# Two output projections and their layer norms, taken over the tokens in two halves instead of at once

## The chip, the core and the metric

The kernel runs on one core of one Trainium2 chip (trn2). The metric is the device time of one execution in microseconds (us). Work is spread over TensorE (PE), VectorE (DVE), ScalarE (ACT), GpSimd (POOL) and the DMA queues, which SyncE (SP) issues here. The engines run on their own instruction lists and meet at semaphores.

## What is computed

Two transformer blocks over 1024 tokens of width 1024, in float32. The part that matters is the end of each of the two layers of the second block:

```python
def mixer_sublayer(x, mem, w_in, w_mem_kv, w_out, main_fn):
    ...
    y = jnp.concatenate([y_main * jax.nn.silu(g_main), y_mem * jax.nn.silu(g_mem)], axis=-1)
    return y @ w_out                      # (1024 x 1536) @ (1536 x 1024)

def second_block(...):
    for layer in range(2):
        if layer == 1:
            k_sh, v_sh, cum_sh = shared_kv(x, w_kv_shared, b_forget)   # x @ w_kv_shared first
        y = mixer_sublayer(x, mem, w_in[layer], w_mem_kv[layer], w_out[layer], main_fn)
        x = layer_norm(ALPHA * x + y, ln_g[layer], ln_b[layer])        # over the 1024 features
```

## The kernel before

Activations lie feature-major in SBUF: 128 features by 1024 tokens is one tile, so a layer norm over the features needs sums over partitions, which PE makes. Every float32 operand is kept as two parts, `hi` and `lo` (names `whi`/`wlo` for weights, `Yb` for the input of the output projection, `Hb` for x), and each product is three matmuls (`mm3`, L327 to L329). A matmul moves 512 tokens, so a weight block of 128x128 is used for two groups of three matmuls.

Weights come as one stream of panels of 128x1024 (eight 128x128 blocks). SP loads panel q into `raw[q % 2]` once panel q-2 is split (`load_panel`, L371). POOL splits it into `whi[q % 2]` and `wlo[q % 2]` (`split`, L672 and L674) once PE is done with panel q-2 (`panel_done`). PE waits for `split`. So the buffers are two deep at each of the three steps, and POOL is at most one panel ahead of the one that PE uses.

`out_proj(l)` appears once in each engine's program. PE (from L1118) makes eight output tiles of 128 features by 1024 tokens from 12 panels; a tile takes 12 blocks, so tiles end in the middle or at the end of a panel (semaphores `out_mid` and `panel_done`). Tile t goes to PSUM pair `G[t % 2]`, and PE may start tile t only when tile t-2 has been taken out (`g_free`). Ahead of it DVE makes the twelve tiles of `Yb_lo` (L1794), and tile 0 waits for them one by one (`yb_lo`).

DVE (from L2191) takes each tile out of PSUM into `Z` and adds ALPHA * x. From tile 3 on, x less a shift row is prepared one tile ahead (`ahead`, L2210 and L2212), so that the take-out is one addition. Then come a running sum (`add_sum`) and a running sum of squares (`add_square`), ACT making the squares. For one tile n of 3 to 6, DVE's list is in this order:

```python
tt(Z[:, n, :], g, Z[:, n, :], ALU.add, free)     # take-out, reads PSUM and SBUF
add_sum(n)                                       # two SBUF inputs
ahead(n + 1)                                     # two instructions, two SBUF inputs each
add_square(n)                                    # two SBUF inputs
```

After tile 7 the norm follows: PE sums over the partitions (L1145), DVE makes mean and variance, ACT the root, PE spreads them to rows (L1151), ACT copies the rows to SBUF (`acc`, `rs`), and DVE and ACT go over the eight tiles: `centred`, `scaled`, ACT's gain and bias, and in layer 0 the split into `Hb_hi` (ACT) and `Hb_lo` (`low`, DVE). In layer 1 ACT's result is stored (`out<-Z`). After layer 0 PE goes on with `token_values(0)`, the shared values: for each of four panels, eight token tiles of 128 tokens (`VORDER`), each to its own PSUM bank, each needing `Hb` of two feature tiles; it waits for `ap_lo`.

The order of instructions on each engine is that of the program text; nothing reorders it.

Of the kernel before, what the change touches and what calls it, by code (L numbers as in the profile page):

```python
# [40 lines left out]
for _name, _w in (("c", 8), ("cc", 8), ("ada_b", 48), ("n1", 8), ("n2", 8), ("b_gate", 16), ("qng", 2),  # L41
# [7 lines left out]
          ("mem", 16), ("mlp", 64), ("pool", 20), ("mem1", 8), ("out1", 12), ("foxv", 4), ("forget", 1), ("foxw", 4), ("fox", 24), ("mem2", 8), ("out2", 12))  # L49
P0 = {}  # L50
_n = 0
for _name, _w in PANELS:
# [3 lines left out]
NP = _n + STREAM_GAP  # L56
# [4 lines left out]
         ("mem1", 16), ("out1", 8), ("mem2", 16), ("out2", 8))  # L61
# [63 lines left out]
VORDER = (tuple(range(8)), (2, 3, 4, 5, 6, 7, 0, 1))  # L125
# [5 lines left out]
def build(nc, d, out, upto=99, dbg=None):  # L131
    ctx = ExitStack()
    with ctx:
# [227 lines left out]
        def sp_program(sp):  # L361
            def load_panel(stage, per, i, j):

                if isinstance(i, int):
                    j, i = j + per * i, 0
                n = P0[stage] + LEAD + j
                q = n + per * i

                sp.wait_ge(S("split"), q - 1)
                for to, of in placed(raw[n % 2], q) if isinstance(i, int) else [(raw[n % 2][:, :], d["w"][q + STREAM_GAP])]:  # L370
                    sp.dma_start(to, of).then_inc(S(f"loaded{n % 2}"), 16)  # L371

            def stream(q):

                if q < P0["gates"]:
                    return 16 + q
                if q < P0["mem"]:
                    return 16 + STREAM_GAP + q
                return STREAM_GAP + q if q >= P0["mlp"] else q - P0["mem"]

            def placed(buf, q):
# [17 lines left out]
                if q < P0["foxv"] or q >= P0["mem2"]:  # L399
                    return [(buf[:, :], d["w"][stream(q)])]  # L400
                w0 = P0["foxv"] + STREAM_GAP
                q += STREAM_GAP
                if q == P0["forget"] + STREAM_GAP:
                    return [(buf[:, :], d["w"][w0])]
                if q < P0["fox"] + STREAM_GAP:
                    n, a = (q - w0, w0 + 3) if q < w0 + 4 else (q - w0 - 5, w0 + 19)
                    return [(buf[:, :].rearrange("p (t c) -> p t c", t=4), d["w"][a:a + 13:4].rearrange("t p c -> p t c")[:, :, 256 * n:256 * n + 256])]
                m = q - STREAM_GAP - P0["fox"]
# [183 lines left out]
            def out_proj(l):  # L592
                st = f"out{l + 1}"
                for j in range(12):
                    load_panel(st, 12, 0, j)
# [53 lines left out]
            if on("out2"):  # L649
                out_proj(1)  # L650
                for k in range(KT):
                    sp.wait_ge(S("ln2_out"), k + 1)
                    sp.dma_start(out[k], Z[:, k, :]).then_inc(S("out_stored"), 16)
                sp.wait_ge(S("out_stored"), 16 * KT)
# [4 lines left out]
        def pool_program(gp):  # L659
# [55 lines left out]
            for stage, per, n in (("mem1", 4, 2), ("out1", 6, 2), ("foxv", 4, 1), ("forget", 1, 1), ("foxw", 4, 1), ("fox", 24, 1), ("mem2", 4, 2),  # L715
                                  ("out2", 6, 2)):
# [8 lines left out]
        def pe_program(pe):  # L725
# [392 lines left out]
            def out_proj(l):  # L1118
                st = f"out{l + 1}"
                have = -1  # L1120
                for t in range(KT):
                    if t == 3:
                        pe.wait_ge(S("ln_sh"), 5 * l + 1)
                        for h in range(2):
                            last = nc.tensor.matmul(ps[:, (4 + h) * HALF:(5 + h) * HALF], onesr[:, :], accr[:, h * HALF:(h + 1) * HALF], start=True, stop=True)
                        last.then_inc(S("ln_sh"), 1)
                    o = pair(pe, st, 8, 0, t)
                    b = 12 * t
                    while b < 12 * t + 12:
                        j = b // 8  # L1130
                        if j != have:
                            wh, wl = panel(st, 12, 0, j)
                            have = j
                        e = min(8 * j + 8, 12 * t + 12)
                        last = blocks(o, wh, wl, Yb[0], Yb[1], range(b - 8 * j, e - 8 * j), b == 12 * t, e == 12 * t + 12, k0=b - 12 * t,
                                      ready=(lambda k: pe.wait_ge(S("yb_lo"), MT * l + k + 1)) if t == 0 else None)
                        if e == 8 * j + 8:
                            done(last)
                        else:
                            last.then_inc(S("out_mid"), 1)  # L1140
                        b = e
                for n, src in enumerate((acc, dsq)):
                    pe.wait_ge(S("ln_acc"), 14 * l + 13 + n)
                    for t in range(KT):
                        last = nc.tensor.matmul(ps[:, (4 + n) * HALF + t:(4 + n) * HALF + t + 1], src[:, P * t:P * t + P], onesf[:, 0:1], start=True, stop=True)  # L1145
                    last.then_inc(S("ln_pe"), 1)
                for n, (b, col_) in enumerate(((6, mean), (4, var))):
                    pe.wait_ge(S("ln_col"), 4 * l + (1, 4)[n])
                    for t in range(KT):
                        c = b * HALF + P * t  # L1150
                        last = nc.tensor.matmul(ps[:, c:c + P], col_[:, t:t + 1].to_broadcast([P, P]), ident[:, :], start=True, stop=True)  # L1151
                    last.then_inc(S("ln_pe"), 1)
# [3 lines left out]
            if on("out1"):  # L1156
                out_proj(0)
            if on("forget"):
# [4 lines left out]
                def token_values(hf):  # L1163
                    st = ("foxv", "foxw")[hf]
                    for n in range(4):
                        wh, wl = panel(st, 4, 0, n)
                        for x, tt in enumerate(VORDER[hf]):
                            if n == 0 and hf == 0 and tt == 4:
                                pe.wait_ge(S("ln_sh"), 5)
                            if n == 0 and hf == 1:  # L1170
                                if tt >= 2:
                                    pe.wait_ge(S("fx_vlo"), 2 * tt + 2)
                                else:
                                    pe.wait_ge(S("logits_read"), 1)
                            for k in range(2):
                                kt = 2 * n + k
                                if hf == 0 and x == 0:
                                    pe.wait_ge(S("ap_lo"), 24 + kt + 1)
# [8 lines left out]
                pe.wait_ge(S("fx_vlo"), 4)  # L1187
# [123 lines left out]
            if on("out2"):  # L1311
                out_proj(1)
# [6 lines left out]
        NORM = {"n1": 0, "latkv": 1, "n2": 2, "ln0": 3, "ln1": 4}  # L1319
        APPLY = {"n1": 0, "n1c": 8, "n2": 16, "ln0": 24, "ln1": 32}  # L1320
# [44 lines left out]
        def act_program(act):  # L1365
# [290 lines left out]
            def out_proj(l):  # L1656
# [7 lines left out]
                act.wait_ge(S("ln_v"), 24 * l + 1)  # L1664
                copy(accr[:, :], Z[:, 0, :], S("ln_sh"))
                act.wait_ge(S("ln_sh"), 5 * l + 2)
                copy(rs[:, 0:T], ps[:, 4 * HALF:6 * HALF], S("ln_sh"), scale=1.0 / P)
                for k in range(KT):
                    if k < 3:
                        act.wait_ge(S("ln_v"), 24 * l + 4 + k)  # L1670
                    else:
                        evicted(act, st, 8, 0, k)
                    if k >= 2:
                        act.wait_ge(S("ln_acc"), 14 * l + 2 * max(k - 2, 1))
                    copy(tmp[k % 2][:, 0:T], Z[:, k, :], S("ln_sq"), ACT.Square)
# [871 lines left out]
```

## Time and profile before

| | |
|---|---|
| Time, median of 3 runs | 3466.75 us (3466.52 to 3469.32) |
| Profiled execution: its time, its span | 3461.23 us, 3459.4 us |
| PE matmul busy | 3136.3 us, 91% of the span |
| DVE busy | 1531.2 us, 44% |
| ACT busy | 911.9 us, 26% |
| POOL busy | 1082.7 us, 31% |
| Mean granted TensorE clock | 0.964 |
| Output projection of layer 0: first to last matmul | from 2287.58 us to 2420.49 us of the span |
| Output projection of layer 1, the norm and the stores | from 3288 us to the end |

Busy shares are averages over stages with different limits. The lines named with an instruction are those of the kernel text. The span runs from the first to the last instruction; the execution's own time is 1.83 us more than the span.

### The profile page before, as it was taken

How to read it: one execution, taken by the hardware profiler on the slowest of the kernel's cores; microseconds unless marked ns; L12 is line 12 of the kernel's file. 1: busy time of each engine (PE TensorE's matmuls, PEld its weight loads, DVE VectorE, ACT ScalarE, POOL GpSimd, SP SyncE). 2: the span in 40 equal slices, each digit the busy share in tenths (PEclk: the TensorE clock that was granted, in tenths of full speed). 3: DMA queues.
4: the chain of work that ended last, by engine and by line, in shares of the span. 5: the costliest groups of instructions: out<-in, count | busy, mean ns of one | idle time of the engine just before them, and what ended most of it. 6: DMA issues, size and time to landing. Idle time of an engine off the chain costs nothing.

```text
span 3459.4 us, 38319 instructions
## 1 busy us (share of the span) xinstructions
PE 3136.3 (91%) x15303; PEld 2619.8 (76%) x15303; DVE 1531.2 (44%) x2168; ACT 911.9 (26%) x1470; POOL 1082.7 (31%) x482
## 2 busy tenths in 40 slices
PE   6979998999889899999999899979899999989797
PEld 6768776888767688888887677658788787867585
DVE  1952212888544331313132343445535656562455
ACT  1322211666212210101011101220334555451212
POOL 0332255000135744434443333214331122211132
PEclk9979998999999999999999999989899999999898
DMA  5343444222142311111111111101241121111012
GB/s 209 129 136 108 170 141 151 65 71 59 67 152 73 122 49 50 49 50 49 50 49 43 49 43 55 43 19 49 64 133 56 50 62 49 56 42 45 24 38 85
DMA packets 114165, 259.37 MB, mean 75 GB/s; under 512 B 46768, under 2 KB 64768, under 8 KB 110032
## 3 DMA queue, kind: packets, MB, share of 16 engines
q1 hardware_dynamic: 113744, 256.95, 22.8%
q8 instruction: 122, 2.00, 0.2%
q14 instruction: 43, 0.35, 0.0%
q10 hardware_dynamic: 256, 0.07, 0.0%
HBM read 214.54 MB, written 42.38 MB: 74 GB/s over the span
## 4 chain that ended last, share of the span: by engine, by line
PE 68%; issue 16%; DVE 8%; POOL 4%; ACT 3%; DMA 1%; POOLq 0%; SPq 0%; DVEq 0%; ACTq 0%
PE ps L327 20%; PE ps L328 20%; PE ps L329 20%; POOL whi L672 2%; PE ps L1272 2%; ACT tmp L1367 2%; DVE tmp L2350 2%; POOL wlo L674 2%; PE ps L769 2%; PE ps L1258 1%; DVE Z L1797 1%; DVE ETb_lo L1794 1%; DMA adaE<-in_ada 1%; PE ps L1115 1%; DMA raw<-in_w 0%
## 5 line engine op out<-in xcount | busy, mean ns | idle before, releaser
L672 POOL TENSOR_TENSOR whi<-raw,onesf 128x1024 fp32r<-128x1024 f32 x235 | 455.6, 1939 | 2308.2 <-PE ps L329 2229.4
L674 POOL TENSOR_TENSOR wlo<-raw,whi 128x1024 fp32r<-128x1024 f32 x235 | 615.2, 2618 | 18.4
L327 PE MATMUL ps<-Hb_hi,whi 128*128 128x512 f32 x1424 | 569.0, 400 | 18.2 <-DVE Y L2135 5.8
L329 PE MATMUL ps<-Hb_hi,wlo 128*128 128x512 f32 x1424 | 555.8, 390 | 0.0
L328 PE MATMUL ps<-Hb_lo,whi 128*128 128x512 f32 x1424 | 555.3, 390 | 0.0
L327 PEld LDWEIGHTS ps<-Hb_hi,whi 128*128 128x128 f32 x1424 | 268.1, 188 | 75.0 <-issue 18.0
L329 PEld LDWEIGHTS ps<-Hb_hi,wlo 128*128 128x128 f32 x1424 | 267.5, 188 | 57.1
L328 PEld LDWEIGHTS ps<-Hb_lo,whi 128*128 128x128 f32 x1424 | 268.3, 188 | 50.0
L1367 ACT ACTIVATE tmp<-ps 64x256 f32<-64x256 f32 (+1 forms) x120 | 81.6, 680 | 654.4 <-PE ps L329 584.8
L1367 ACT ACTIVATE tmp<-tmp,mx 128x1280 f32<-128x1280 f32 (+2 forms) x192 | 187.1, 974 | 107.0 <-DVE mx L2350 89.2
L327 PE MATMUL ps<-Uhi,whi 128*128 128x512 f32 x512 | 199.2, 389 | 0.0
L328 PE MATMUL ps<-Ulo,whi 128*128 128x512 f32 x512 | 199.2, 389 | 0.0
L329 PE MATMUL ps<-Uhi,wlo 128*128 128x512 f32 x512 | 199.2, 389 | 0.0
L327 PE MATMUL ps<-Yb_hi,whi 128*128 128x512 f32 x384 | 151.3, 394 | 36.0 <-DVE Yb_lo L1794 36.0
L2095 DVE SCALAR_TENSOR_TENSOR X<-ps,modx,X 128x1024 f32<-128x1024 f32 x32 | 41.1, 1284 | 286.5 <-PE ps L329 286.5
L1797 DVE TENSOR_TENSOR tmp<-tmp 128x1024 f32<-128x1024 f32 x32 | 64.3, 2008 | 202.0 <-ACT tmp L1367 202.0
L328 PE MATMUL ps<-Yb_lo,whi 128*128 128x512 f32 x384 | 150.7, 392 | 0.0
L329 PE MATMUL ps<-Yb_hi,wlo 128*128 128x512 f32 x384 | 150.6, 392 | 0.0
L327 PE MATMUL ps<-Hhi,whi 128*128 128x512 f32 x320 | 127.6, 399 | 9.9 <-DVE Hlo L1331 9.9
L328 PE MATMUL ps<-Hlo,whi 128*128 128x512 f32 x320 | 126.1, 394 | 0.0
L329 PE MATMUL ps<-Hhi,wlo 128*128 128x512 f32 x320 | 126.0, 394 | 0.0
L1258 PE MATMUL ps<-ident,tmp 128*128 128x128 f32 x576 | 88.9, 282 | 28.9 <-ACT tmp L1367 28.8
(403 smaller groups left out, 6088.7 us busy)
## 6 DMA issues: line engine op xcount, KB each, us to landing
raw<-in_w SPq DMA_DIRECT2D x221, 512.0 KB, 3.3
adas<-in_ada SPq DMA_DIRECT2D x16, 1024.0 KB, 4.9
raw<-in_w SPq DMA_DIRECT2D x36, 256.0 KB, 4.0
adaE<-in_ada SPq DMA_DIRECT2D x4, 2048.0 KB, 25.3
gate_d<-gst SPq DMA_DIRECT2D x16, 512.0 KB, 2.9
v_d<-VS SPq DMA_DIRECT2D x2, 4096.0 KB, 14.3
ncB<-cum_d SPq DMA_DIRECT2D x16, 512.0 KB, 3.7
Vx<-v_d SPq DMA_DIRECT2D x16, 512.0 KB, 4.5
```

The lines of the kernel that those rows point to most:

```text
L327: nc.tensor.matmul(o, wh, xh, start=start, stop=False)
L328: nc.tensor.matmul(o, wh, xl, start=False, stop=False)
L329: return nc.tensor.matmul(o, wl, xh, start=False, stop=stop)
L672: nc.gpsimd.tensor_tensor(whi[b][:, 0:w], raw[b][:, 0:w], onesf[:, 0:1].to_broadcast([P, w]), ALU.mult).then_inc(S("split_hi"), 1)
L674: nc.gpsimd.tensor_tensor(wlo[b][:, 0:w], raw[b][:, 0:w], f32(whi[b][:, 0:w]), ALU.subtract).then_inc(S("split"), 1)
L769: last = nc.tensor.matmul(ps[:, c:c + 2], adaE[g][:, n // 2, k, P * (n % 2):P * (n % 2) + P], silc[:, :].rearrange("p (x k) -> p k x", k=K ...
L1258: last = nc.tensor.transpose(ps[:, b + P * (kt - 4 * x):b + P * (kt - 4 * x) + P], tmp[qt % 2][:, P * kt:P * kt + P], ident[:, :])
L1272: last = nc.tensor.matmul(ps[:, 5 * HALF + c0:5 * HALF + CTX], Vx[h % 2][:, kt, :], E[x][:, kt, c0:CTX], start=kt == 0 and x == 0, stop=kt ...
L1367: nc.scalar.activation(dst, src, func, **kw).then_inc(sem, 1)
L1797: nc.vector.tensor_tensor(o, a, b, op).then_inc(sem, 1)
L2095: nc.vector.scalar_tensor_tensor(X1[:, k, :], g, modx[:, 40 + k:41 + k], X1[:, k, :], ALU.mult, ALU.add).then_inc(free, 1)
L2350: nc.vector.tensor_tensor_reduce(tmp[qt % 2][:, c0:c1], ps[:, b:b + c1 - c0], ncB[:, c0:c1], -1.0, col_ if x else 3e38, ALU.add, ALU.min, ...
```

## The change

Both output projections run over the tokens by halves of 512 (`x` = 0, 1). The numbers of panels and tiles double, and the second half's panels are the same weights loaded and split again:

```diff
-... ("out1", 12), ... ("out2", 12))        # PANELS
+... ("out1", 24), ... ("out2", 24))
-... ("out1", 8), ... ("out2", 8))          # TILES
+... ("out1", 16), ... ("out2", 16))
-VORDER = (tuple(range(8)), (2, 3, 4, 5, 6, 7, 0, 1))
+VORDER = ((1, 3, 0, 2, 4, 5, 6, 7), (2, 3, 4, 5, 6, 7, 0, 1))
+BESIDE = {3: (0, 1), 4: (2, 3), 5: (4, 5), 6: (6,), 7: (7,)}
```

A panel now serves 24 matmuls instead of 48. PE's program:

```diff
+                def token_sums(x):          # over the partitions, for 4 token tiles
+                    for n, src in enumerate((acc, dsq)):
+                        pe.wait_ge(S("ln_acc"), 14 * (2 * l + x) + 13 + n)
+                        ... 4 matmuls of 128x1
+                def rows(x, n):             # n = 0 mean, n = 1 inverse deviation
+                    pe.wait_ge(S("ln_col"), 4 * (2 * l + x) + (1, 4)[n])
+                        ... 4 matmuls of 128x128
+                for x in range(2):
+                    X = [y[:, :, HALF * x:HALF * x + HALF] for y in Yb]
                     for t in range(KT):
+                        if t == 3:
+                            shift_row(x)
+                        if x and t == 1:
+                            token_sums(0)
+                        if x and t == 2:
+                            rows(0, 0)
+                            rows(0, 1)
+                        o = pair(pe, st, 16, 0, 8 * x + t)
...
+                yield
+                token_sums(1)
+                yield
+                rows(1, 0)
+                yield
+                rows(1, 1)
+                yield
```

In layer 0 the last three steps stand between the first four token tiles of `token_values(0)`, which belong to half 0 (order 1, 3, 0, 2); the other four wait for half 1 (`ap_lo` 24 + 2 * x + kt + 1 for x = 0 and 4). In layer 1 they follow each other. DVE's program (`first` is the take-out of tiles 0 to 2, all operations are 512 wide):

```diff
+                for x in range(2):
+                    first(x, 0)
+                    if x:
+                        moments(0)
+                    first(x, 1)
+                    if x:
+                        inverse(0)
+                    first(x, 2)
+                    if x:
+                        for k in range(3):
+                            centred(0, k)
...
+                    for n in range(3, KT):
+                        g, free = arrive(x, n)
+                        tt(Z[:, n, c], g, Z[:, n, c], ALU.add, free)
+                        add_sum(x, n)
+                        if n + 1 < KT:
+                            ahead(x, n + 1)
+                        add_square(x, n)
+                        if x:
+                            for k in BESIDE.get(n, ()):
+                                scaled(0, k)
+                                if k + 3 < KT:
+                                    centred(0, k + 3)
+                                if k:
+                                    low(0, k - 1)     # layer 0 only
+                low(0, KT - 1)
+                moments(1)
+                inverse(1)
...
```

ACT's program has the same order: squares of half 0, `factors(0)` (root and the two row copies), squares of half 1 with gain and bias (and `Hb_hi`) of half 0 beside them by `BESIDE`, `factors(1)`, the rest of half 1. SP loads 24 panels instead of 12 in each projection and stores the result in 16 pieces of 256 KB instead of 8 of 512 KB, the first eight as soon as half 0 is ready. POOL splits the 24 panels with the same two instructions each. The twelve `Yb_lo` instructions at the start stay 1024 wide.

## Rows read from the trace of the kernel before

**Rows 1.** The page's chain of work that ended last, by engine.

```profile
PE 68%; issue 16%; DVE 8%; POOL 4%; ACT 3%; DMA 1%; POOLq 0%; SPq 0%; DVEq 0%; ACTq 0%
```

**Rows 2.** Busy time by stretch: us and (instructions) of each engine, clock, DMA.

```profile
2287.00:2298.00 11.00, 10.42 (x37) 8.49 (x38) 11.00 (x11) 3.23 (x4) 0.00 (x0) 0.78 0.00 0
2298.00:2421.00 123.00, 122.88 (x543) 101.40 (x541) 53.54 (x39) 9.53 (x9) 51.35 (x22) 1.00 0.17 48
2421.00:2450.00 29.00, 14.90 (x70) 13.35 (x71) 20.64 (x20) 11.62 (x12) 5.10 (x2) 0.69 0.09 20
3421.00:3460.00 39.00, 12.93 (x67) 11.93 (x65) 25.16 (x23) 14.49 (x14) 5.10 (x2) 0.64 0.31 122
```

**Rows 3.** PE in order of time, projection of layer 0 and what follows: start, us.

```profile
2287.58 0.77 PE L327 MATMUL ps<-Yb_hi,whi 128*128 128x512 f32 x1 [17.98 <-DVE Yb_lo L1794]
...
2420.49 0.39 PE L329 MATMUL ps<-Yb_hi,wlo 128*128 128x512 f32 x1
2424.05 2.75 PE L1145 MATMUL ps<-onesf,acc 128*128 128x1 f32 x16 [3.18 <-DVE acc L1797]
2427.34 3.57 PE L1145 MATMUL ps<-onesf,dsq 128*128 128x1 f32 x16 [0.54 <-DVE dsq L1797]
2430.77 3.76 PE L1151 MATMUL ps<-ident,stat 128*128 128x128 f32 x16
2436.07 2.05 PE L1151 MATMUL ps<-ident,stat_pool 128*128 128x128 f32 x16 [1.54 <-DVE stat_pool L2265]
2445.20 0.77 PE L327 MATMUL ps<-whi,Hb_hi 128*128 128x512 f32 x1 [7.08 <-DVE Hb_lo L1794]
...
2450.16 0.63 PE L327 MATMUL ps<-whi,Hb_hi 128*128 128x512 f32 x1
```

**Rows 4.** Groups of instructions from 2287 to 2421 us, shapes apart: busy, mean ns.

```profile
L674 POOL TENSOR_TENSOR wlo<-raw,whi 128x1024 fp32r<-128x1024 f32 x11 | 29.8, 2708 | 0.9
L672 POOL TENSOR_TENSOR whi<-raw,onesf 128x1024 fp32r<-128x1024 f32 x11 | 21.6, 1961 | 116.8 <-PE ps L329 116.8
L1794 DVE TENSOR_TENSOR Yb_lo<-Y,Yb_hi 128x1024 fp32r<-128x1024 f32 x12 | 13.7, 1220 | 0.0
```

**Rows 5.** POOL in order of time, in the projection of layer 1.

```profile
3334.14 1.90 POOL L672 TENSOR_TENSOR whi<-raw,onesf 128x1024 fp32r<-128x1024 f32 x1 [5.65 <-PE ps L329]
3336.11 2.39 POOL L674 TENSOR_TENSOR wlo<-raw,whi 128x1024 fp32r<-128x1024 f32 x1
3345.47 1.90 POOL L672 TENSOR_TENSOR whi<-raw,onesf 128x1024 fp32r<-128x1024 f32 x1 [6.97 <-PE ps L329]
3347.45 3.25 POOL L674 TENSOR_TENSOR wlo<-raw,whi 128x1024 fp32r<-128x1024 f32 x1
3356.36 1.90 POOL L672 TENSOR_TENSOR whi<-raw,onesf 128x1024 fp32r<-128x1024 f32 x1 [5.65 <-PE ps L329]
```

**Rows 6.** DVE in order of time, beside the last three rows of POOL.

```profile
3345.52 2.93 DVE L1797 TENSOR_TENSOR Z<-Z,rs 128x1024 f32<-128x1024 f32 x1
3348.37 3.41 DVE L1797 TENSOR_TENSOR dsq<-tmp 128x1024 f32<-128x1024 f32 x1
3351.70 1.21 DVE L1797 TENSOR_TENSOR acc<-acc,Z 128x1024 f32<-128x1024 f32 x1
3352.84 1.21 DVE L2210 SCALAR_TENSOR_TENSOR Z<-Hb_hi,rs 128x1024 f32<-128x1024 f32 x1
...
3356.36 1.22 DVE L1797 TENSOR_TENSOR Z<-ps,Z 128x1024 f32<-128x1024 f32 x1
```

**Rows 7.** Narrower operations of DVE and ACT over the whole span: busy, mean ns.

```profile
L1794 DVE TENSOR_TENSOR ETb_lo<-ps,ETb_hi 128x512 fp32r<-128x512 f32 x64 | 42.7, 688 | 15.9 <-ACT ETb_hi L1367 15.9
L1367 ACT ACTIVATE rs<-ps 128x512 f32<-128x512 f32 x8 | 4.7, 590 | 7.3 <-PE ps L329 7.2
```

**Rows 8.** ACT and DMA at the end of layer 1; weight loads of the page.

```profile
3452.51 3.51 ACT L1367 ACTIVATE Z<-Z,cols 128x1024 f32<-128x1024 f32 x3 [1.03 <-DVE Z L1797]
raw<-in_w SPq DMA_DIRECT2D x221, 512.0 KB, 3.3
```

More of the change, by code:

```diff
@@ L1119, in out_proj @@
                 st = f"out{l + 1}"
-                have = -1
[L1121 to L1141, printed above, removed]
@@ L1142, in out_proj, with shift_row @@
-                for n, src in enumerate((acc, dsq)):
-                    pe.wait_ge(S("ln_acc"), 14 * l + 13 + n)
-                    for t in range(KT):
[L1145 to L1152, printed above, removed]
+                def shift_row(x):
+                    pe.wait_ge(S("ln_sh"), 8 * l + 2 * x + 1)
+                    nc.tensor.matmul(ps[:, 4 * HALF:5 * HALF], onesr[:, :], accr[:, HALF * x:HALF * x + HALF], start=True, stop=True).then_inc(S("ln_pe"), 1)
@@ L1156, in pe_program @@
             if on("out1"):
-                out_proj(0)
+                norm = out_proj(0)
+                next(norm)
             if on("forget"):
@@ new lines, in low @@
+                def low(x, k):
+                    if l:
+                        return
+                    c, _ = half(x)
+                    dve.wait_ge(S("ap_hi"), APPLY[f"ln0{x}"] + k + 1)
+                    sub(Hb[1][:, k, c], tmp[k % 2][:, c], Hb[0][:, k, c], S("ap_lo"))
+                for x in range(2):
+                    first(x, 0)
[8 more added lines that the diff above has]
+                            centred(0, k)
+                    dve.wait_ge(S("ln_v"), 16 * (2 * l + x) + 3)
+                    dve.wait_ge(S("ln_sh"), 8 * l + (2, 6)[x])
+                    shifted(x, 0)
+                    shifted(x, 1)
+                    add_sum(x, 1)
+                    shifted(x, 2)
+                    add_square(x, 1)
+                    add_sum(x, 2)
+                    ahead(x, 3)
+                    add_square(x, 2)
+                    for n in range(3, KT):
+                        g, free = arrive(x, n)
+                        c, m = half(x)
+                        dve.wait_ge(S("ln_v"), 16 * m + 2 * n + 2)
+                        tt(Z[:, n, c], g, Z[:, n, c], ALU.add, free)
[10 more added lines that the diff above has]
+                                    low(0, k - 1)
@@ L2293, in dve_program @@
+                low(1, KT - 1)
             if on("mem1"):
```

298 lines of the change are left out of this document (174 added, 124 removed).

## Prediction, made before the changed kernel ran

> **What bounds the kernel now.** I read the page's chain first: PE holds 68% of it [rows 1], so TensorE sets most of the time. Then the windows around the edit. In the 123 us of the projection PE has work without a gap, at the full clock, while POOL works 51.4 us and DVE 53.5 us [rows 2]. In the 29 us behind it and in the last 39 us PE is half idle, and the clock falls to 0.69 and 0.64 [rows 2]: these are the two norm tails, the only thing near the edit that a change can win.
>
> The time line of PE gives their size [rows 3]. From the first matmul (2287.58) to the end of the last issue (2420.49 + 0.23) are 133.1 us. 12 panels of 48 matmuls are 576; at 5.45 us for 24 (0.227 us each, the rate that is left when some 2 us of cold start and shift row are taken off) they make 131 us. PE then works steadily again only at 2450.16, with six matmuls (1.4 us) done before: 28 us lost. In layer 1 from 3421.3 to 3459.4: 38.1 us to the end.
>
> The view that decides is DVE beside POOL, in order of time. POOL's `wlo` takes 2.39 us alone and 3.25 with DVE at work [rows 5]. DVE's additions of two SBUF inputs take 1.14 us from start to start, but 2.93 and 3.41 us when POOL works [rows 6]. The ends fit to the tenth: `whi` runs to 3347.37, DVE's addition that started at 3345.52 ends at 3348.45, 1.08 us later; `wlo` ends at 3350.70, DVE's next at 3351.78, again 1.08 later [rows 5, 6]. So the two don't run at once: they take turns, one instruction each. An addition that reads PSUM beside `whi` took its plain 1.22 us at 3356.36 [rows 5, 6]. Before, this cost nothing, since POOL needs 4.4 us of each 10.9 us panel.
>
> **The prices.** POOL: 24 panels by 1.90 + 2.39 = 4.3 us are 103 us per projection, for 12 panels before 52. PE uses up a panel in 5.45 us, so POOL alone keeps pace, with 1.1 us to spare. Loading a panel takes 3.3 us [rows 8] and has one split's time (4.4 us or more) before it is needed, so the 12 added loads of 512 KB lie hidden; uncovered they would cost 3.3 us for the first only.
>
> DVE: a 512-wide operation isn't in the trace with two SBUF inputs. The upper bound is 0.69 us, the one with a PSUM input [rows 7]; the lower is half of 1.14, 0.57. I take 0.60 alone, 0.55 in a turn between two POOL instructions, 0.65 for a take-out from PSUM. ACT: 0.59 [rows 7] for half of 1024, where 0.5 would be half: small, and ACT has room.
>
> Port turns per projection: 103 (POOL), 12 Yb_lo by 1.08 = 13, and DVE's two-input instructions: per half 3 (second step of the take-out), 3 shifted, 7 sums, 7 sums of squares, 10 ahead = 30, and 16 of the norm (24 in layer 0 with `low`): 92 and 108 by 0.55 = 51 and 59. In all 167 and 175 us. Before the same sum was 52 + 13 + 46 or 54 by 1.08 = 115 and 123, in a window (first matmul to last DVE step) of 167 and 181 us. So the port that DVE and POOL take turns at goes from two thirds full to all of it. The change can't win much even if it packed perfectly.
>
> **How it runs.** I went through the four lists by hand, with PE 5.45 us a panel, POOL 1.90 and 2.39, DVE as above; t counts from the first matmul of the projection.
>
> Start: tile 0 needs twelve Yb_lo. They come 1.14 us apart [rows 4], and a block now lasts 0.68 us instead of 1.36, so PE waits for DVE. Panel 0 is done at 8.8; POOL then splits panel 2 and takes two turns between the last four Yb_lo. Tile 0 ends at 17.5, where 12 blocks and the cold start would be 9.7: +7.8.
>
> Half 0: POOL is busy nearly throughout, so DVE gets two turns in a panel, three in a tile (1.5 panels, 8.2 us), and it needs four: add_sum, two ahead, add_square. It falls behind. Tiles 0 to 2 leave ten turns behind the take-out of tile 2 (its second step, 3 shifted, 2 sums, 2 squares, 2 ahead), due before the take-out of tile 3, for which tile 5 waits: PE stands from 50.5 to 54.8: +4.3. While PE stands POOL has nothing to split, and DVE catches up; tiles 6 and 7 just fit. Half 0 ends at 79.3.
>
> Between the halves: token_sums(0) is due after tile 8, at 88.2. DVE then still has the end of half 0 before it (take-out of tile 7 at 91.5, the last sum at 92.1). PE's sums were 2.75 and 3.57 us for eight token tiles [rows 3], half of that now, and are over at 95.8: +7.6. The rows: half of 3.76 and 2.05 us plus a wait for the inverse, which is queued behind the take-out of tile 9: +3.9.
>
> Half 1: to the four turns of a tile come scaled, centred and low, twice in tiles 3 to 5: 9, 10 and 9 turns where POOL leaves three. PE stands before tiles 13 and 14 of 16 for psum pairs, 6.5 us each: +13. Tile 15 meets a DVE that has caught up but is then 14 turns behind once more. The last matmul comes 36.6 us later than before, at t = 170 in layer 0, and some 2.4 us earlier than that in layer 1, which has no low.
>
> Tail of layer 0: behind the last matmul DVE still has those 14 turns with POOL's last split between them. The last sums are in at 184.9, PE's sums end at 187.5, rows at 190.8 and 193.2 (token tiles between), the first Hb_lo of half 1 at 196.4, the second at 198.3. PE has done 27 matmuls (6.2 us) there, so it lost 28 - 6 = 22 us, against 28 before: -6. Layer 0: 36.6 - 6.3 = +30. Tail of layer 1: sums at 183, rows at 186.5, the last scaled at 195.5, ACT 0.8, and as before 3.4 us from ACT's end (3456.0 [rows 8]) to the end of the span: 199.7 against 171.2 before: +28.5. Standing 3 us or more has also brought the 1.2 GHz clock back (0.63 us instead of 0.39 at 2450.16) [rows 3], about 1.5 us each time; since DVE and POOL gain what PE loses, I count +3 in all.
>
> Sum: 30 + 28.5 + 3 = +61 on the profiled execution's 3461.23 us. This execution lies 5.5 us below the median of the runs; a difference holds on either, so 3466.75 + 61 = 3528; I take 3526, since the waits in the walk were rounded up.
>
> The Trainium skill has a rule on this, and it speaks against the change: SBUF — State Buffer, section "Who interferes with whom", says that a DVE instruction with two SBUF inputs contends with a GpSimd instruction that reads SBUF, that the later one waits for the whole of the earlier one, and that one SBUF input does not contend. The rows on both sides agree. If the take-outs from PSUM contended too, 16 more turns of 0.55 us would be added per projection, some 18 us in both.
>
> **Rivals.**
> A, forecast: turns at the port, DVE behind, PE waits for PSUM pairs: +61, own range +35 to +90.
> B, the lists pack well: PE's waits are filled, and only the port's sum counts. Window 167 or 175 us plus about 6 us in which nobody can use it (panel 0 to 2, wait for PE at t = 15 to 20) and the 3.4 us of stores: +5 in layer 1 and 0 to +10 in layer 0; with the start's +7.8 half seen in each, +13 to +23 (3480 to 3490). For it: DVE does catch up whenever PE stands. Against: POOL has no work in just these waits, so port time is lost.
> C, other side, one mechanism: 512-wide steps slip into POOL's 1.1 us of slack per panel and DVE keeps up. It decides at DVE finishing a tile's work within 8.17 us. Then the costs are 3.6 (Yb_lo paces tile 0: 13.3 for 9.7), 5.2 of PE's inserted sums and rows, 1.5 of waiting: +10.3; the tails shrink to half a norm: -16 in layer 0, -13 in layer 1. Together -8: 3459. For it: the tails are really long. Against: 4.3 + 3 by 0.55 us a panel is more than 5.45.
> D, POOL becomes PE's bound: a turn of DVE costs POOL 0.87 us as the 1024-wide one did (3.25 less 2.39) whatever its width. A panel takes 4.3 + 1.7 = 6.0 us, 0.6 by 22 by 2 = 26 us more than A: +87, 3554. Against: the wait should shrink with the width.
>
> **How the numbers follow.** A 0.64, B 0.15, C 0.08, D 0.08, and 0.05 that gains and costs meet within 0.2% (7 us, about what a measurement tells from no change). Range: from the upper part of B (+19) to D (+87): 3486 to 3554. Outside lie C, no change, half of B's chance, and a little of A's and D's ends, 0.2 to 0.25 in all. Faster by over 0.2%: 0.05 (most of C), same 0.06, slower 0.89.
>
> **What would show it.** Two groups of 24 splits between the first and last Yb matmul instead of 12; POOL busy around 100 us of some 170. DVE's 512-wide two-input steps averaging well over 1 us in the projection. PE waiting for Yb_lo inside tile 0, for DVE's take-out (Z<-ps) several times by 4 to 7 us, and about 7 us before the sums of half 0. First to last matmul of the projections 160 to 180 us instead of 133. The tail of layer 0 about as long as before, that of layer 1 some 7 us shorter. The prediction is wrong if PE has no gaps before tiles 5, 13 and 14, or if 512-wide steps beside POOL take under 0.8 us.

## Result and profile after

| | before | after |
|---|---|---|
| Time, median (range), same chip | 3468.03 us (3466.52 to 3473.71) | 3508.01 us (3505.46 to 3509.36) |
| Ratio to before | | 1.0111 [1.0094, 1.0129] |
| Profiled execution: its time, its span | 3461.23, 3459.4 us | 3509.36, 3507.5 us |
| First to last Yb matmul, layer 0 / layer 1 | 133.1 / 132.7 us | 166.9 / 163.1 us |
| First Yb matmul of layer 0 to that of layer 1 | 1001.1 us | 1025.1 us |
| First Yb matmul of layer 1 to the end of the span | 170.8 us | 190.2 us |
| POOL busy, whole span | 1082.7 us | 1199.3 us |

The kernel became 40 us slower. In the profiled executions the spans differ by 48.1 us: 24.0 in layer 0, 19.4 in layer 1, and 4.7 ahead of the first Yb matmul of layer 0. Those 4.7 us are in stages that the change doesn't touch: over all kernels of this document that matmul starts anywhere from 2284.7 to 2294.1 us. So I compare by the two stages.

The page's chain of the changed kernel, by engine: beside [rows 1] PE has given 6 points away, 3 to issue and 2 to DVE.

```profile
PE 62%; issue 19%; DVE 10%; POOL 4%; ACT 3%; DMA 1%; POOLq 0%; SPq 0%; DVEq 0%; ACTq 0%
```

Windows of the changed kernel (columns as in [rows 2]): start, rest of the projection of layer 0, its tail, end of layer 1.

```profile
2292.00:2303.00 11.00, 10.06 (x30) 6.62 (x30) 11.00 (x11) 2.90 (x4) 1.85 (x1) 0.79 0.00 0
2303.00:2459.00 156.00, 139.07 (x582) 111.81 (x581) 116.17 (x97) 23.25 (x36) 109.22 (x46) 0.93 0.24 75
2459.00:2485.00 26.00, 16.69 (x68) 13.38 (x67) 20.08 (x30) 10.54 (x16) 4.99 (x2) 0.74 0.20 43
3468.00:3507.50 39.50, 17.18 (x68) 14.67 (x68) 31.16 (x39) 12.72 (x19) 10.91 (x5) 0.71 0.42 147
```

In the second line POOL is busy 109.2 us of 156 (51.4 of 123 before) and DVE 116.2 (53.5), though DVE's arithmetic grew only by the norm of one half. PE is no longer busy throughout: 139 of 156, at a granted clock of 0.93 instead of 1.00.

PE in order of time, layer 0 of the changed kernel: the places where it waited, and the four inserted steps.

```profile
2309.34 0.50 PE L331 MATMUL ps<-Yb_hi,whi 128*128 128x512 f32 x1 [1.01 <-POOL wlo L688]
2343.44 0.50 PE L331 MATMUL ps<-Yb_hi,whi 128*128 128x512 f32 x1 [3.39 <-DVE Z L1869]
2378.33 0.94 PE L1145 MATMUL ps<-onesf,acc 128*128 128x1 f32 x8
2379.13 1.03 PE L1145 MATMUL ps<-onesf,dsq 128*128 128x1 f32 x8
2388.33 1.05 PE L1152 MATMUL ps<-ident,stat 128*128 128x128 f32 x8
2391.22 1.20 PE L1152 MATMUL ps<-ident,stat_pool 128*128 128x128 f32 x8 [1.84 <-DVE stat_pool L2332]
2424.18 0.79 PE L331 MATMUL ps<-Yb_hi,whi 128*128 128x512 f32 x1 [5.34 <-DVE Z L1869]
2448.33 0.79 PE L331 MATMUL ps<-Yb_hi,whi 128*128 128x512 f32 x1 [4.97 <-DVE Z L1869]
2466.99 1.87 PE L1145 MATMUL ps<-onesf,acc 128*128 128x1 f32 x8 [6.38 <-DVE acc L1869]
2480.77 0.66 PE L331 MATMUL ps<-whi,Hb_hi 128*128 128x512 f32 x1 [2.43 <-DVE Hb_lo L1866]
```

A row starts where its wait ends. Three stops wait for DVE's take-out (`Z`): before tiles 5, 13 and 15 (180, 468 and 540 Yb matmuls lie ahead of them). Behind each the clock is at 1.2 GHz for a while (granted 0.59 from 2424 to 2431 us, 0.60 from 2448 to 2455); the matmuls behind the later two show 0.79 and 0.63 us instead of 0.39.

The groups of layer 0's projection, shapes apart (busy, mean ns), answer to [rows 4]:

```profile
L688 POOL TENSOR_TENSOR wlo<-raw,whi 128x1024 fp32r<-128x1024 f32 x23 | 60.9, 2647 | 1.8
L686 POOL TENSOR_TENSOR whi<-raw,onesf 128x1024 fp32r<-128x1024 f32 x23 | 50.2, 2183 | 95.4 <-PE ps L333 95.4
L1869 DVE TENSOR_TENSOR dsq<-dsq,tmp 128x512 f32<-128x512 f32 x10 | 18.4, 1845 | 0.0
L1869 DVE TENSOR_TENSOR acc<-acc,Z 128x512 f32<-128x512 f32 x11 | 17.6, 1596 | 0.3
L1869 DVE TENSOR_TENSOR Z<-ps,Z 128x512 f32<-128x512 f32 x9 | 6.1, 683 | 2.6 <-PE ps L333 2.6
```

Two SBUF inputs cost 1.6 to 1.85 us on average, one of them in PSUM 0.68, of the same width. The turns can be read one by one where DVE is behind, near tile 15, POOL first, then DVE:

```profile
2455.97 2.72 POOL L688 TENSOR_TENSOR wlo<-raw,whi 128x1024 fp32r<-128x1024 f32 x1
2459.39 2.32 POOL L686 TENSOR_TENSOR whi<-raw,onesf 128x1024 fp32r<-128x1024 f32 x1 [0.71 <-PE ps L333]
2461.79 2.67 POOL L688 TENSOR_TENSOR wlo<-raw,whi 128x1024 fp32r<-128x1024 f32 x1
2456.36 2.87 DVE L2294 SCALAR_TENSOR_TENSOR Z<-Hb_hi,rs 128x512 f32<-128x512 f32 x1
2459.88 2.38 DVE L1869 TENSOR_TENSOR dsq<-dsq,tmp 128x512 f32<-128x512 f32 x1
2462.18 2.82 DVE L1869 TENSOR_TENSOR tmp<-Z,rs 128x512 f32<-128x512 f32 x1
```

POOL's three end at 2458.69, 2461.71 and 2464.46, DVE's at 2459.23, 2462.26 and 2465.00: each time 0.54 or 0.55 us later, one 512-wide step. POOL pays 0.3 us for such a turn (2.72 and 2.67 against 2.39 [rows 5]).

### The profile page after: what moved, and what is told of

Same layout as the page of the kernel before. It is cut to its first block, busy times and chain, and to the rows that moved or that the text cites. A ratio compares the mean times of both kernels' runs of the same rounds, so it can differ in the third digit from the quotient of the medians.

```text
span 3507.5 us, 38701 instructions
## 1 busy us (share of the span) xinstructions
PE 3164.1 (90%) x15303; PEld 2630.7 (75%) x15303; DVE 1638.4 (47%) x2292; ACT 924.4 (26%) x1520; POOL 1199.3 (34%) x530
## 4 chain that ended last, share of the span: by engine, by line
PE 62%; issue 19%; DVE 10%; POOL 4%; ACT 3%; DMA 1%; POOLq 0%; SPq 0%; DVEq 0%; ACTq 0%
PE ps L331 19%; PE ps L332 18%; PE ps L333 18%; POOL whi L686 2%; PE ps L1313 2%; DVE Z L1869 2%; POOL wlo L688 2%; ACT tmp L1409 2%; DVE tmp L2463 2%; PE ps L783 1%; PE ps L1299 1%; DVE acc L1869 1%; DVE ETb_lo L1866 1%; DMA adaE<-in_ada 1%; PE ps L908 0%
## 5 line engine op out<-in xcount | busy, mean ns | idle before, releaser
L686 POOL TENSOR_TENSOR whi<-raw,onesf 128x1024 fp32r<-128x1024 f32 x259 | 511.8, 1976 | 2248.4 <-PE ps L333 2169.5
L688 POOL TENSOR_TENSOR wlo<-raw,whi 128x1024 fp32r<-128x1024 f32 x259 | 676.0, 2610 | 20.3
L331 PE MATMUL ps<-Yb_hi,whi 128*128 128x512 f32 x384 | 161.2, 420 | 65.9 <-DVE Yb_lo L1866 38.0
L1409 ACT ACTIVATE tmp<-tmp,mx 128x1280 f32<-128x1280 f32 (+2 forms) x192 | 187.1, 974 | 108.7 <-DVE mx L2463 90.7
L331 PEld LDWEIGHTS ps<-Yb_hi,whi 128*128 128x128 f32 x384 | 76.5, 199 | 95.1 <-issue 40.8
```

Of the source, the lines that this page charges most:

```text
L331: nc.tensor.matmul(o, wh, xh, start=start, stop=False)
L686: nc.gpsimd.tensor_tensor(whi[b][:, 0:w], raw[b][:, 0:w], onesf[:, 0:1].to_broadcast([P, w]), ALU.mult).then_inc(S("split_hi"), 1)
L688: nc.gpsimd.tensor_tensor(wlo[b][:, 0:w], raw[b][:, 0:w], f32(whi[b][:, 0:w]), ALU.subtract).then_inc(S("split"), 1)
L1409: nc.scalar.activation(dst, src, func, **kw).then_inc(sem, 1)
```

## Experiments

"Changed" below is the changed kernel, "before" the one before. Times are medians; each ratio is to before on the same chip. The two stages: P0 / P1 are first to last Yb matmul in layers 0 and 1; L0 and L1 the two stage times of the table above (changed: P 166.9 / 163.1, L 1025.1 / 190.2; before: P 133.1 / 132.7, L 1001.1 / 170.8). Before's own median beside these runs was 3464 to 3466 us for 1 to 5, 3471 for 6 to 9 and 3467 for 10 to 12, so a difference of two medians of different groups can be off by a few us; the stage times, from the profiled executions, are the closer comparison.

| kernel | us | ratio | P0 / P1 | L0 / L1 |
|---|---|---|---|---|
| 1 a_tiny | 3445.29 | 0.9947 [0.9930, 0.9964] | 140.7 / 140.7 | 990.9 / 161.4 |
| 2 b_split_twice | 3480.30 | 1.0050 [1.0034, 1.0067] | 139.8 / 139.3 | 1011.3 / 177.4 |
| 3 a_beside_end | 3506.11 | 1.0121 [1.0101, 1.0141] | 159.3 / 157.9 | 1025.0 / 187.5 |
| 4 a_yb_halves | 3508.98 | 1.0134 [1.0117, 1.0151] | 167.6 / 166.0 | 1025.0 / 191.4 |
| 5 b_norm_halves | 3465.36 | 0.9996 [0.9986, 1.0006] | 133.2 / 133.9 | 998.4 / 170.9 |
| 6 a_split_512 | 3497.93 | 1.0089 [1.0063, 1.0115] | 159.3 / 159.0 | 1020.6 / 184.5 |
| 7 a_narrow_squares | 3503.20 | 1.0100 [1.0075, 1.0125] | 163.3 / 158.1 | 1021.5 / 187.1 |
| 8 a_one_input_squares | 3498.30 | 1.0090 [1.0064, 1.0115] | 163.4 / 158.1 | 1021.6 / 187.1 |
| 9 a_act_hi | 3464.95 | 0.9990 [0.9978, 1.0002] | 150.0 / 147.5 | 1001.1 / 170.6 |
| 10 a_psum | 3474.44 | 1.0022 [1.0013, 1.0031] | 150.4 / 149.5 | 1010.4 / 171.4 |
| 11 a_psum_act_hi | 3463.35 | 0.9993 [0.9984, 1.0002] | 149.9 / 147.9 | 1001.1 / 168.8 |
| 12 b_act_hi | 3471.07 | 1.0013 [1.0004, 1.0022] | 133.1 / 132.7 | 1004.5 / 174.1 |

**1, changed without POOL's work.** The loads and waits stay, the split is 8 columns wide (the weights' other columns are left unsplit).

```diff
-split(P0[stage] + SPLIT_LEAD + j, i, per)
+split(P0[stage] + SPLIT_LEAD + j, i, per, 8 if stage in ("out1", "out2") else PW)
```

> The changed kernel, with POOL's two split instructions of the 48 panels of both output projections cut from 1024 to 8 columns (so most of the split weights of these panels are stale; panels, loads, semaphores and PE's matmuls are all there). Theory A, the port that POOL and DVE take turns at: the waits of PE for DVE's take-outs (3.4, 5.4 and 5.0 us in layer 0, 3.4, 5.4 and 3.2 in layer 1) vanish, and with them the cold clock behind them; the projection takes about 143 us instead of 167 and 163; the whole time falls by 45 to 55 us to 3455 to 3465, a little under the kernel before. Theory B, DVE's own work and the order of its list: the waits stay, and the time stays above 3495. Theory C, POOL alone too slow for PE's 5.45 us a panel: only the waits for wlo (1.0 us twice) vanish, 3505.

All of the loss is gone, and the kernel is 19 us faster than before; it came out 10 us under theory A's range. DVE's groups in layer 0's projection are at their plain duration:

```profile
L1869 DVE TENSOR_TENSOR acc<-acc,Z 128x512 f32<-128x512 f32 x11 | 7.6, 690 | 0.3
L1869 DVE TENSOR_TENSOR dsq<-dsq,tmp 128x512 f32<-128x512 f32 x11 | 7.5, 685 | 0.0
```

PE waited in no place over 0.7 us up to the end of the projection. What turns the halves into a loss is the split beside DVE. Without it they are about 10 us a layer ahead of before (990.9 for 1001.1, 161.4 for 170.8), with DVE's longer list and the doubled loads in it. That is an upper bound for what the halves are worth: before still makes its own 12 splits a projection, and it wasn't run without them.

**2, before with POOL's work doubled.** Each of the 24 splits of the projections is made twice.

```diff
+for _ in range(2): whi = raw * onesf; wlo = raw - whi      # only in stages out1, out2
```

> The kernel before, with each of the 24 splits of the two output projections made twice in a row on POOL: the doubled splitting alone, with no halves. POOL is then busy 8.7 of each 10.9 us. Theory A: in a tile of 16.3 us POOL takes 12.9 and DVE's four two-input steps 4.3 of the shared port, 17.2 together, so DVE falls behind by 1 us a tile and its steps average above 2 us; PE begins to wait late in the projection and the tails get longer: +10 to +25 us, 3478 to 3493. Theory B, the port doesn't matter: 0 to +3 us.

Theory A's range held (+16 us), but by another wait than in the changed kernel: here POOL is the one that PE waits for, four times a projection, and the tails hardly grew (3.5 us in layer 0, none in layer 1).

```profile
2358.69 0.47 PE L327 MATMUL ps<-Yb_hi,whi 128*128 128x512 f32 x1 [1.59 <-POOL wlo L680]
2370.93 0.50 PE L327 MATMUL ps<-Yb_hi,whi 128*128 128x512 f32 x1 [1.08 <-POOL wlo L680]
```

With 1024-wide steps beside them the splits average 2.9 (`wlo`) and 2.35 us (`whi`), 10.5 a panel of 10.9. The doubled splitting alone costs 6.7 and 6.6 us in the two projections, where the changed kernel lost 33.8 and 30.4. DVE has half as many steps here, each twice as wide, and so needs half the turns.

**3, the norm of half 0 not beside tiles 11 to 15 but behind tile 15.**

```diff
-BESIDE = {3: (0, 1), 4: (2, 3), 5: (4, 5), 6: (6,), 7: (7,)}
+BESIDE = {7: (0, 1, 2, 3, 4, 5, 6, 7)}
```

> The changed kernel with BESIDE = {7: all eight}: the norm's steps for half 0 stand behind tile 7 of half 1 instead of between its tiles. Theory A: the wait before tile 14 of 16 goes (5 us and 3 us, and 1.5 us of cold clock), the one before tile 13 stays, but 16 or 24 steps of 0.6 us now lie in the tail, ahead of the moments of half 1: 3505 to 3525. Rival, the interleaving is what costs: 3495 or less.

As theory A had it, nothing is gained: the projection ends 7.6 us sooner (the second late stop is gone), and PE then waits 8.65 us for the first token tiles. DVE's norm steps of half 0 were only put off; behind the last matmul they take their plain 0.68 us each.

```profile
2462.21 0.77 PE L331 MATMUL ps<-whi,Hb_hi 128*128 128x512 f32 x1 [8.65 <-DVE Hb_lo L1866]
```

**4, Yb_lo by halves**, the second twelve behind the take-outs of tiles 0 and 1.

```diff
-for f in range(MT): Yb_lo(f)                    # 1024 wide
+for f in range(MT): Yb_lo(0, f)                 # 512 wide
+first(0, 0); Yb_lo(1, 0..5); first(0, 1); Yb_lo(1, 6..11)
```

> The changed kernel with the twelve Yb_lo instructions made by halves too: 512 wide for half 0 ahead of tile 0, those of half 1 behind the take-outs of tiles 0 and 1, where DVE is idle. Theory: tile 0 is no longer paced by DVE (3.5 us a layer) and the first split of the projection doesn't wait for the row of Yb_lo (1 us): 7 to 9 us less, 3499 to 3501. Rival: the time is given back at the wait before tile 5, since the port is full: 0 to 2 us less.

The theory (7 to 9 us less) missed and the rival (0 to 2 us less) comes nearer: nothing was gained. The start became faster (the shift row came at t = 27.2 instead of 30.9 us, t counted from the first Yb matmul), and the next take-out later. The wait moved to tile 4:

```profile
2324.55 0.80 PE L331 MATMUL ps<-Yb_hi,whi 128*128 128x512 f32 x1 [3.54 <-DVE Z L2288]
```

**5, before with only its norm by halves**, projection untouched: sums of squares, rows and norm steps in pieces of 512.

```diff
+PIECES = [(x, 2 * n + k) for n in range(4) for x in range(2) for k in range(2)]
```

> The kernel before with its projection untouched (12 panels, split once), and only the norm behind it by token halves: sums of squares, mean and deviation rows and their copies for tokens 0 to 511 first, then centred, scaled, gain and bias and the split of x in pieces of 512 tokens, in the order half 0 of features 0 and 1, half 1 of features 0 and 1, half 0 of features 2 and 3, and so on; the token tiles wait for their own half. Theory: both tails get shorter since the row copies and the first pieces come earlier, with no work added for POOL: the first Hb_lo some 9 us earlier in layer 0, the end some 3 us earlier in layer 1: 8 to 15 us less, 3453 to 3460. Rival: the tail is paced by DVE's 24 and 16 steps, which are no shorter by halves: 0 to 4 us less.

Missed: 8 to 15 us less were expected, and the time is before's; it lies in the rival's range (0 to 4 us less), though not for the rival's reason alone (a tail paced by DVE's steps). The norm started sooner, as meant: PE's steady row begins at 2446.13, 19.6 us behind the last Yb matmul, where it was 29.7 before [rows 3]. Most of that was given back further on; 2.7 us of layer 0's stage are left. POOL, DVE and PE some 10 to 27 us later:

```profile
2456.77 13.93 POOL L675 TENSOR_TENSOR whi<-raw,onesf 128x1024 fp32r<-128x1024 f32 x1 [24.54 <-PE ps L329]
```
```profile
2468.27 0.68 DVE L1833 TENSOR_TENSOR tmp<-Z,rs 128x512 f32<-128x512 f32 x1
2469.29 4.71 DVE L1830 TENSOR_TENSOR Hb_lo<-tmp,Hb_hi 128x512 fp32r<-128x512 f32 x2 [0.34 <-ACT Hb_hi L1381]
```
```profile
2473.50 0.80 PE L327 MATMUL ps<-whi,Hb_hi 128*128 128x512 f32 x1 [6.00 <-POOL wlo L677]
```

`whi` (1.9 us of work) was given the port at 2470.70 - 1.90 = 2468.80 us, just when DVE's unbroken row of 512-wide steps ended (2468.95) because it had to wait for ACT. PE then stood 6 us for the panel. POOL had come at 2456.77; 20 steps of DVE, 0.60 us from start to start, began after that and went ahead of it.

**6, the same splits in four instructions of 512 columns.**

```diff
-tensor_tensor(whi[b][:, 0:w], ...); tensor_tensor(wlo[b][:, 0:w], ...)
+tensor_tensor(whi[b][:, s_], ...) for both halves s_ of w; the same for wlo
```

> The changed kernel, with each split of the two projections' stages made by four POOL instructions of 512 columns instead of two of 1024: the same weights, the same bytes, but DVE may take the port between any two of them. Turns by instruction (my theory): DVE gets up to four turns a panel, six a tile, and needs four in half 0, so the wait before tile 5 (3.4 us) goes and those before tiles 13 and 14 shrink to under 2 us; POOL pays for more turns and PE waits for wlo in small pieces. First to last Yb matmul 150 to 158 us instead of 167 and 163, total 3480 to 3498 us. Rival, the port is full and only the sum of port time counts, however it is cut: within 4 us of the changed kernel, 3504 to 3512 us.

At the upper end of the theory's range, 10 us better than changed (4.5 and 5.7 in the two stages); the projections, 159 us, missed the theory's 150 to 158. The wait before tile 5 is gone, six waits of 0.4 to 1.2 us for `wlo` came in half 0 of layer 0, and in half 1 three more of them came and two for the take-out stayed, of 1.0 and 4.8 us. The theory's "under 2 us" for the last missed; finer turns help DVE, but POOL pays for them (1.37 and 1.52 us for half a panel, 5.8 for a panel that PE uses up in 5.45).

```profile
L694 POOL TENSOR_TENSOR wlo<-raw,whi 128x512 fp32r<-128x512 f32 x46 | 69.1, 1521 | 1.8
L689 POOL TENSOR_TENSOR whi<-raw,onesf 128x512 fp32r<-128x512 f32 x46 | 62.1, 1369 | 69.2 <-PE ps L333 69.2
```

**7 and 8, changed with 12 of 14 additions of squares on 8 columns** (most of the sum of squares is left out): in 7 as additions of two SBUF inputs, in 8 as `tensor_scalar` of one.

```diff
-tt(dsq[:, c], dsq[:, c], tmp[n % 2][:, c], ALU.add, S("ln_acc"))
+tt(dsq[:, w], dsq[:, w], tmp[n % 2][:, w], ALU.add, S("ln_acc"))        # 7, w: 8 columns
+nc.vector.tensor_scalar(dsq[:, w], tmp[n % 2][:, w], 1.0, None, ALU.mult)   # 8
```

> The changed kernel with twelve of the fourteen additions to the running sum of squares in each projection done on 8 columns instead of 512 (that part of the sum of squares is left out; the instructions, their order and their two SBUF inputs stay). Turns by instruction: an addition of 8 columns still has to wait for POOL's instruction to end, so DVE is as far behind as before; it only gives back its own 0.5 us each, some 2 to 3 of which lie ahead of each of PE's waits. Waits before tiles 5, 13 and 14 each 0 to 1.5 us shorter, total 3498 to 3506 us. Rival, only port time counts: 12 by 0.55 us less in each projection, all seen in the time: 3492 to 3496 us, and the same time as when the additions leave the port altogether.

> The counterpart: the same twelve additions are replaced by DVE instructions with one SBUF input, on 8 columns (the sum of squares is left out here too). Turns by instruction: one turn a tile less for DVE; it needs three in half 0, which is what POOL leaves it, so the wait before tile 5 goes, and in half 1 each tile ends up to 2.3 us earlier on DVE: waits before tiles 13 and 14 down to 0 to 3 us. Total 3482 to 3495 us, at least 8 us below the kernel with narrow additions. Rival, only port time counts: equal to the kernel with narrow additions within 2 us.

7 came within the theory's total; its waits in layer 0 are 0.4 to 0.6 us shorter, but in layer 1 the one before tile 15 (3.2 us) is gone altogether, more than the theory's 1.5. 8 missed, and for a reason that its own rows show: both kernels have the same stage times to 0.1 us (their profiled executions differ by 8.3 us, all of it ahead of the first Yb matmul), and 8's instructions of one input take the port too:

```profile
L2318 DVE TENSOR_SCALAR dsq<-tmp 128x8 f32<-128x8 f32 x10 | 13.3, 1326 | 0.0
```

1.33 us on average for 8 columns, at least 0.16 and at most 2.36: almost all of it waiting for POOL. 7's additions, two inputs on 8 columns, average 1.32 us. So this pair doesn't tell turns from port time, as the turn was not taken away; it shows that 8 columns wait as long as 512 (1.32 less 0.16, and 1.85 less 0.68 in the changed kernel, are both 1.16 us). The Trainium skill (SBUF — State Buffer, section "Who interferes with whom") says that `tensor_scalar` can enter a mode that uses the port pair shared with GpSimd, if its operands meet that mode's conditions. The wait of 1.33 us agrees with it; the mode itself is not seen in a trace.

**9, ACT makes whi in the projections**, POOL only wlo; nothing left out. Before each square ACT's list gets the copies that can be due.

```diff
+copy(whi[b][:, :], raw[b][:, :], S("split_hi"))      # ACT, after loaded and panel_done
```

> The changed kernel, but in the two projections ACT makes whi (a copy of one SBUF input, 1024 columns) and POOL makes wlo alone; nothing is left out. ACT's copies are placed in its list where their panel can be free. Turns at the port: POOL holds it 24 by 2.4 = 58 us instead of 103, DVE has room for all its steps, no wait for PSUM pairs over 1 us. First to last Yb matmul 141 to 150 us, total 3448 to 3465 us. Rival, ACT is the new wait: it runs its list in order, so a copy stands behind a square or a gain-and-bias step that waits for DVE, the split comes late and PE waits for wlo: 3480 us or more.

At the upper end of the theory's range, 43 us under the changed kernel (24.0 and 19.6 in the two stages). No stop for DVE's take-out is left; the projection's 150 us hold waits for `wlo` in half 1 (0.4, 3.7, 1.4 and 1.0 us).

**10, the same instructions with an operand in PSUM.** ACT writes the squares of tiles 1 to 7 to two free PSUM banks, and `centred` and `scaled` of half 0 read their row there. POOL's work is untouched, nothing is left out.

```diff
-copy(tmp[k % 2][:, c], Z[:, k, c], S("ln_sq"), ACT.Square)
+copy(squares[k % 2] if k else tmp[0][:, c], Z[:, k, c], S("ln_sq"), ACT.Square)
-tt(dsq[:, c], dsq[:, c], tmp[n % 2][:, c], ALU.add, S("ln_acc"))
+tt(dsq[:, c], squares[n % 2], dsq[:, c], ALU.add, S("ln_acc"))
```

> The changed kernel with DVE's operands moved, nothing left out: ACT writes the squares of tiles 1 to 7 of each half to two free PSUM banks, and centred and scaled of half 0 read their row from PSUM instead of SBUF. So 14 additions and 16 norm steps per projection have one SBUF input and one from PSUM, the form that took its plain 0.69 us beside POOL in every trace so far; POOL's splits stay as they are. Turns at the port: DVE needs three a tile in half 0, which is what POOL leaves, and 3 to 5 in half 1. Wait before tile 5 under 1 us, those of half 1 together under 6 us, projections 147 to 156 us, total 3466 to 3488 us. Rival, it is not the two SBUF inputs that make DVE wait: within 5 us of the kernel with narrow additions, 3496 us or more.

As expected, 34 us under the changed kernel (14.7 and 18.8 in the two stages), with the same instructions on the same engines. DVE's groups beside POOL:

```profile
L1871 DVE TENSOR_TENSOR acc<-acc,Z 128x512 f32<-128x512 f32 x10 | 16.4, 1640 | 0.3
L1871 DVE TENSOR_TENSOR dsq<-ps,dsq 128x512 f32<-128x512 f32 x10 | 6.8, 679 | 0.0
L1871 DVE TENSOR_TENSOR Z<-Z,ps 128x512 f32<-128x512 f32 x8 | 5.3, 678 | 0.0
```

The addition of squares fell from 1845 ns to 679, the sum of values, left in SBUF, kept 1640 (1596 in the changed kernel). One wait of 3.8 us for the take-out remains.

**11, 9 and 10 together; 12, before with 9's edit as a control** (in 12 ACT copies 12 panels a projection).

> The same, and ACT makes whi in the two projections as in the run before; nothing left out. Turns at the port: POOL holds it 24 by 2.4 us, DVE's steps all fit, and ACT's list is no longer kept waiting by a late DVE, so PE's waits for wlo in half 1 (8 us in sum with ACT's whi alone) fall to under 3 us. Projections 141 to 146 us, tails as with the tiny splits: total 3444 to 3456 us, faster than both kernels. Rival, ACT itself is late, whatever DVE does, since its copies of 1024 columns stand behind squares and gain-and-bias steps: waits as before, 3460 to 3468 us.

> The kernel before, with ACT making whi in the two projections' stages. It is the control: if the relieved port is worth something only where the port is full, this stays within 4 us of the kernel before (12 turns fewer of 24, none of which PE waits for). Rival, the relief alone is worth as much without the halves: 5 us or more faster than before, and then what the halves with it bring is that much less theirs.

11 missed (3444 to 3456 us were expected) and came in its rival's range: 3463.35 us, not to be told from before. ACT, POOL and PE at the largest wait:

```profile
2406.15 0.82 ACT L1410 ACTIVATE tmp<-tmp,cols 128x512 f32<-128x512 f32 x1 [2.65 <-DVE tmp L1892]
2408.91 1.04 ACT L1410 ACTIVATE whi<-raw 128x1024 fp32r<-128x1024 f32 x1
```
```profile
2410.03 2.61 POOL L689 TENSOR_TENSOR wlo<-raw,whi 128x1024 fp32r<-128x1024 f32 x1 [8.91 <-ACT whi L1410]
```
```profile
2412.69 0.50 PE L331 MATMUL ps<-Yb_hi,whi 128*128 128x512 f32 x1 [3.77 <-POOL wlo L689]
```

The weight copy stands behind the first two gain-and-bias steps of half 0, which wait for DVE's `scaled`; POOL has nothing to do for 8.9 us. It is the order of ACT's list now. In 12 the relief alone brings nothing: it is 4.5 us slower than before, a little outside the 4 us that were expected for a control, with 3.4 and 3.3 in the two stages. 9 and 11 lie 6 to 8 us under 12. That is the halves' share only if ACT's copies cost the three kernels the same, which no run shows. No kernel with the whole work in it beats the one before by more than a measurement tells.

## Why the prediction was right, and where its sizes were off

The forecast was +61 us, measured +40, inside the range of +19 to +87; the mechanism was A. That DVE's two-input steps and POOL's splits take turns, that this made DVE late for the PSUM pairs, and that the loss hangs on it, is shown from both sides: 3445 us without POOL's part (1), 3465 with less of it (9), and 3474 with 30 of DVE's 92 or 108 turns a projection taken from the port (10).

Its steps in layer 0, with t from the first Yb matmul:

| step | predicted | measured |
|---|---|---|
| start, up to panel 2 | +7.8 us | +3.5, then 1.0 of waiting for wlo |
| wait before tile 5 | 4.3, from t = 50.5 to 54.8 | 3.4, from t = 47.8 to 51.2 |
| token_sums(0) | +7.6 | +1.7, no wait |
| rows | +3.9 | +3.8 |
| two waits in half 1 | 6.5 and 6.5, before tiles 13, 14 | before tiles 13, 15: 5.3 and 5.0 (layer 1: 5.4 and 3.2) |
| last matmul, against before | +36.6 (layer 1 34.2) | +33.8 (30.4) |
| tail behind it | -6.3 (layer 1 -5.7) | -9.8 (-11.0) |
| slower clock, both layers | +3 | 7.9 + 5.8 within the projections |

That the last matmul came within 3 us of the forecast is partly luck. The steps ahead of it add up to 36.6 us in the forecast and to about 24 in the trace; the slower clock, 7.9 us there, fills most of the difference.

**Start.** I had two turns of POOL between the last `Yb_lo`. There were none. DVE and POOL at the start of layer 0:

```profile
2290.88 13.71 DVE L1866 TENSOR_TENSOR Yb_lo<-Y,Yb_hi 128x1024 fp32r<-128x1024 f32 x12
2301.15 5.20 POOL L686 TENSOR_TENSOR whi<-raw,onesf 128x1024 fp32r<-128x1024 f32 x1 [50.76 <-PE ps L333]
```

`whi` ends at 2306.35, so its 1.90 us of work began at 2304.45, with the end of the whole row (2304.59). So POOL did not hold up tile 0, and panel 2 came late instead, a wait that the walk did not have. The stop before tile 5 begins 2.7 us sooner than forecast. C's bound for this step (3.6) was the better one.

**Between the halves.** token_sums(0) was the largest miss: DVE began the take-out of tile 7 at 2370.39 and had the last sum of half 0 in at 2375.57, t = 83.3, ahead of PE's arrival at t = 86.1, where my walk had 92.1. I let DVE lag through tiles 6 and 7; in fact it then waited 2.96 us for PE.

**Tails.** The sums of half 1 were due 14 turns behind the last matmul by my walk. DVE's last two ended at t = 174.7 (2466.93) and 175.5 and not at 184.9: it was behind before the take-out of tile 15, not after it, as most of half 0's norm had been done while PE stood. That made the tails 3.5 and 5 us shorter than I had them.

**Clock.** Some 50 and 38 matmuls of the two projections ran at 1.2 GHz (0.43 us apart instead of 0.227), against 10 and 7 before: (40 + 31) by 0.2 us are 14 us, of which I had 3. Each of the six stops of 3.2 to 5.4 us had 7 to 14 slow matmuls behind it, on top of its own length. In layer 0 seven more came behind the inserted rows (granted clock 0.57 from 2392 to 2396 us), where PE had waited no longer than 1.84 us; in layer 1 none did. The clock is the one large term that I had too small; the terms that were too large, the start, the sums, the waits of half 1 and the tails, outweigh it.

**Rivals.** B, packing: its 3480 to 3490 needed waits that fill themselves; they stayed, and even with the splits in smaller pieces (6) it is 3498. C: decided at DVE finishing a tile in 8.17 us; experiment 1 takes away what prevents that and comes near C's picture, with projections of +7.6 and +8.0 (C had 10.3) and tails of -17.8 and -17.4 (16 and 13). D: a 512-wide turn cost POOL 0.3 us, not 0.87; refuted by the rows near tile 15.

Open is whether a better order of ACT's list would take 11 down to experiment 1's 3445 us; it wasn't tried. Open, too, is how much of experiment 1's gain over before is the halves', and why in b_norm_halves' layer 1 the projection is 1.2 us longer, which takes back the 1.1 us of its tail.

## What to carry to other kernels

Cutting a stage in half to start its successor sooner also doubles what is done once per stage, here the weight split, and the price was not its own time (POOL kept pace) but the port that it shares with DVE: count the turns at it, engine by engine and tile by tile, before moving work beside a matmul row. Where it is full, an operand in PSUM or a copy on ACT is worth more than narrower instructions (10 and 9, 34 and 43 us, against 7, 5 us). And where an engine takes work from another's list, look at what it is queued behind.

## What the runs showed of the hardware that I had not expected

An unbroken row of DVE instructions with two SBUF inputs can keep the port against a POOL instruction that comes while it runs: 5.20 us for a `whi` of 1.90 at the start of the changed projections, 13.93 us in experiment 5, each time until DVE stopped or changed to something else. The one-for-one turns show up where DVE's step itself had waited for POOL [rows 5, 6]. But POOL can also get in behind a single step that had not waited, as in the changed kernel, where `whi` took 0.42 us more than its 1.90 and DVE's next step had to wait for it:

```profile
2348.13 2.32 POOL L686 TENSOR_TENSOR whi<-raw,onesf 128x1024 fp32r<-128x1024 f32 x1 [5.89 <-PE ps L333]
2348.01 0.69 DVE L2296 SCALAR_TENSOR_TENSOR Z<-Hb_lo,Z 128x512 f32<-128x512 f32 x1
2348.62 2.38 DVE L1869 TENSOR_TENSOR dsq<-dsq,tmp 128x512 f32<-128x512 f32 x1
```

What decides between these is not shown here.

A DVE `tensor_scalar` of 8 columns with one SBUF input waits for POOL like one with two inputs (means 1.33 and 1.32 us, 0.16 the shortest), while in the projections of the changed kernel and of experiment 10 no step of 512 columns with one of its two inputs in PSUM took over 0.69 us.
